# Latent attention: eight of 26 projection units of the next head reserved for places in front of the first output matmuls of the query groups

## The reference, cut to what matters

```python
q = (rmsnorm(c_q, q_norm_g) @ w_uq).reshape(B, S, 8, 128 + 64)      # c_q has 512 features
kv = (rmsnorm(c_kv, kv_norm_g) @ w_ukv).reshape(B, S, 8, 128 + 128)  # c_kv has 256 features
q_nope, q_pe = q[..., :128], q[..., 128:]      # q_pe, k_pe get rotary positions
k_nope, v = kv[..., :128], kv[..., 128:]
s = (q_nope @ k_nope.T + q_pe @ k_pe.T) * 192 ** -0.5               # per head, causal
o = softmax(where(kpos <= qpos, s, -inf)) @ v                        # S = 4096, 8 heads
```

## Time and profile before

| | us |
|---|---|
| median of 3 runs (lowest to highest) | 4792.64 (4781.29 to 4819.37) |
| the profiled execution, its own time | 4795.18 |
| its span, slowest core (core 1) | 4793.2 |
| spans of all cores | 4772.3 to 4793.2 |
| stage 2 in the span, about | 345 to 1027 |

### The profile page before, as it was taken

One profiled execution on the slowest core, in us unless ns is written; L12 is line 12 of the kernel. 1 busy time (PEld: TensorE's weight loads), 2 busy tenths in 40 slices (PEclk: granted clock), 3 DMA queues, 4 the chain that ended last, 5 costly groups with the idle time before them and its releaser, 6 DMA issues.

```text
span 4792.3 us, 76088 instructions; the slowest of 8 cores (4772.3 to 4793.2 us)
## 1 busy us (share of the span) xinstructions
PE 4430.4 (92%) x28892; PEld 2344.1 (49%) x28892; DVE 1692.0 (35%) x2919; ACT 1443.1 (30%) x2431; POOL 124.8 (3%) x211
## 2 busy tenths in 40 slices
PE   5979999975969999599999999999999999999998
PEld 4756666643545555344454444444444444444443
DVE  5632333200212231222566021663124661226641
ACT  4536666630111212112332012432113330123320
POOL 0000000000000000000000000000000000000000
PEclk8879999987989999799999999999999999999999
DMA  8539899799998342154334464445554445644443
GB/s 259 197 66 104 108 108 108 99 176 141 178 160 161 91 115 58 47 170 141 133 137 141 163 220 158 150 154 167 183 195 149 152 145 174 220 158 150 153 137 140
DMA packets 166439, 703.14 MB, mean 147 GB/s; under 512 B 19972, under 2 KB 38692, under 8 KB 150180
## 3 DMA queue, kind: packets, MB, share of 16 engines
q1 hardware_dynamic: 135636, 508.39, 32.3%
q0 software_dynamic: 30448, 189.90, 24.9%
HBM read 783.21 MB, written 138.94 MB: 192 GB/s over the span
## 4 chain that ended last, share of the span: by engine, by line
PE 86%; DMA 4%; DVE 3%; ACT 2%; issue 2%; another core or an unknown queue 2%; SPq 1%; DVEq 0%; POOL 0%; ACTq 0%; POOLq 0%
PE wide L260 79%; PE bank L260 7%; DMA cs<-cosT 2%; ACT pt L269 1%; SPq L74 1%; DVE tm L275 1%; DMA mo<-MOs 1%; DMA wuq<-w_uq 0%; DVE on L484 0%; DVE zacc L272 0%; DMA h<-Hs 0%; ACT zacc L269 0%; DMA x<-xT 0%; PE tbank L695 0%
## 5 line engine op out<-in xcount | busy, mean ns | idle before, releaser
L260 PE MATMUL wide<-h,w 128*128 128x512 bf16 (+1 forms) x11360 | 2104.3, 340 | 141.4 <-DMA h<-Hs 140.1
L260 PEld LDWEIGHTS wide<-h,w 128*128 128x128 bf16 x11360 | 954.5, 97 | 1241.1 <-issue 162.3
L260 PE MATMUL wide<-hid,wd 128*128 128x512 bf16 x2752 | 602.5, 379 | 0.0
L275 DVE SCALAR_TENSOR_TENSOR ac<-u,vecs_sb,ac 128x512 f32<-128x512 f32 x688 | 513.7, 747 | 36.9 <-DVE ac L275 1.4
L269 ACT ACTIVATE ac<-u,vecs_sb 128x512 f32<-128x512 f32 x344 | 280.0, 814 | 648.5 <-DVE u L272 648.4
L260 PEld LDWEIGHTS wide<-hid,wd 128*128 128x128 bf16 x2752 | 269.2, 98 | 324.7
L272 DVE TENSOR_TENSOR u<-wide,rs 128x512 f32<-128x512 f32 (+1 forms) x430 | 250.9, 584 | 382.3 <-PE wide L260 337.0
L272 DVE TENSOR_TENSOR x<-wide,x 128x512 f32<-128x512 f32 (+1 forms) x144 | 89.8, 632 | 739.2 <-PE wide L260 739.2
L536 ACT ACTIVATE pt<-wide,vecs_sb 128x1024 bf16<-128x1024 f32 x256 | 284.5, 1114 | 215.4 <-PE wide L260 204.8
L260 PE MATMUL wide<-qn,kh 128*128 128x512 bf16 (+1 forms) x960 | 311.6, 340 | 4.7 <-DVE vh L447 3.8
L260 PE MATMUL wide<-qp,kpe 128*128 128x512 bf16 (+1 forms) x960 | 309.5, 340 | 2.7 <-issue 2.7
(11 more groups left out here) (140 smaller groups left out, 2939.5 us busy)
## 6 DMA issues: line engine op xcount, KB each, us to landing
w<-w_up_bf SPq DMA_DIRECT2D x344, 512.0 KB, 3.2
h<-Hs SPq DMA_DIRECT2D x64, 1024.0 KB, 14.0
w<-w_gate_bf SPq DMA_DIRECT2D x128, 512.0 KB, 3.3
wd<-w_dn_bf SPq DMA_DIRECT2D x64, 704.0 KB, 4.1
w_up_bf<-w_up POOLq DMA_DIRECT2D x43, 1024.0 KB, 13.7
wd<-w_dn_bf SPq DMA_DIRECT2D x64, 672.0 KB, 3.9
x<-xT SPq DMA_DIRECT2D x16, 2048.0 KB, 9.8
w<-w_out_bf SPq DMA_DIRECT2D x64, 512.0 KB, 3.2
```

The source lines that it names most:

```text
L260: P.op("pe", lambda E: E.matmul(out_ap, lhsT=lhsT_ap, rhs=rhs_ap, start=start, stop=stop, **kw), reads=reads, writes=[out_T])
L275: P.op("dve", lambda E: E.scalar_tensor_tensor(out=out_ap, in0=in0, scalar=scalar, in1=in1, op0=op0, op1=op1), reads=reads, writes=[out_T])
```

## The change

The pace now treats 8 of the 26 units as kept back: it pops while more than 8 are left and as if there were 18 of them. Each entry of `pend` gets a flag, whether it is the first `stage_b` of a query group (or the halo's); in front of one so flagged, up to two units are popped from `fill`. The loop behind the halo step stays as it is.

```diff
-                while fill and len(fill) * total > 26 * (total - stepn):
+                while fill and len(fill) > 8 and (len(fill) - 8) * total > 18 * (total - stepn):
                     fill.pop(0)()
                 while len(pend) > LAG:
-                    pend.pop(0)()
+                    opens, b_step = pend.pop(0)
+                    if opens:
+                        for _ in range(2):
+                            if fill:
+                                fill.pop(0)()
+                    b_step()
...
-                    pend.append(stage_b)
+                    pend.append((kb == 0, stage_b))
...
-            pend.append(halo_b)
+            pend.append((True, halo_b))
             step_end()
             while fill:
                 fill.pop(0)()
             cur = nxt
         while pend:
-            pend.pop(0)()
+            pend.pop(0)[1]()
```

## The result

The changed kernel takes 4898.3 us (median of 6 runs, the lowest 4891.6) against 4806.0 for the kernel before in the same session (lowest 4781.3; its median before the prediction was 4792.6). The ratio is 1.0208, with a 95% interval of 1.0169 to 1.0247: 2.1% slower, forecast were 4900 us and +2.2%. The profiled executions took 4892.6 us against 4795.2, +97, where the sum of the prediction has +108; that the median of 4898.3 comes within 2 us of the 4900 is in part luck.

The account below looks back on a forecast made before the run. TensorE, busy 92% of 4793.2 us, was taken as the bound. 4795 + 55 (burst) + 31 (clock) + 22 (openings) = 4903, forecast as 4900 us, +2.2%; range 4880 to 4925, or 4858 to 4925 including the clock-full case.

Parts of the forecast that it names:

- The count of pops: In the two pop loops: 8 of the units are never taken off the reserve and remain behind each halo step.
- 1, the burst: Behind the halo step of 7 heads: eight left-over units through bank 6, seven uncovered holes of 1.11 us each, +55 us.
- 2, the clock: TensorE's clock falls to half inside and behind each head-end burst, 4.4 us per head, +31 us (bounds 0 to 49).
- the rival of 4870 us: In the head-end bursts the clock stays full, as no single hole is long; 4870 us by median, chance 0.20.
- 3, the openings: At each head's five openings the second unit waits for the first's cast behind the division; +22 us (bounds -21 to +30).
- steps 3 and 13: Openings at these steps of a head: holes grow by 1.1 and 0.7 us, to about 1.1 us each.
- steps 2 and 25: Openings at these steps of a head: holes of 1.27 us become 1.56 and 1.5, +0.3 and +0.2 us.
- 4, what costs nothing: Ordinary steps without a unit, buffers, transfers, queues and VectorE's count of work: no added time.
- Clock full: Rival: TensorE's clock stays full through the head-end bursts; 4872 us, by median 4870, chance 0.20.
- Openings that absorb their units: Rival: paired units lie in existing holes at the openings, none left for a burst; 23 us less, 4770, chance 0.03.
- The smaller loss: Rival: round trip partly hidden or fewer left-over units, openings and half the burst; 4845 us down to no change, chance 0.07.

Follow-up runs that it names:

- e3: Changed kernel with the units behind the halo step rotating over bank 6 and the four score banks; ratio to before 1.0105, stage 2 729.0 us.
- e8: Rerun of the changed kernel with four unused 512-column matmuls added in each of a burst's seven holes; stage 2 765.2 us against 786.7 in the changed kernel.
- e1: Changed kernel without the pops at the openings, leaving the burst alone; stage 2 764.1 us, 81.4 over the kernel before, no ratio.
- e6: Changed kernel with the reserve reduced by each pair, none popped at the halo and none left behind its step; ratio to before 1.0056, stage 2 715.3 us.
- e7: Changed kernel with the old pace and one unit at an opening only where the pace put none; ratio to before 0.9978, stage 2 675.1 us.
- e5: Kernel before, units and pace unchanged, with each group's first output matmuls held back one step more; ratio 0.9962, stage 2 668.9 us.
- e2: Changed kernel with the old pace, nothing kept back, pops at the openings staying; stage 2 721.9 us, 39.2 over the kernel before, no ratio.
- e4: Changed kernel with four 512-column matmuls of unused result added in each of a burst's seven holes; stage 2 764.3 us, 81.6 over the kernel before.

## Why the prediction was right, point by point

- **The count of pops.** Eight value units stand behind each of seven halo steps. It decided the sign and most of the size, and it came from the two conditions alone.
- **1, the burst, +55.** 49 waits of 0.97 us by the profile's counting, each with the 0.16 by which a matmul's record ends behind its last issue: 1.13 x 49 = 55. e3 shows that it is the single bank.
- **2, the clock, +31.** The total was right, its split was not. Taken were a fall 5 us into the burst, 3.4 at the earliest, 1.7 us lost inside and 2.65 behind. Over the 47 bursts whose eight units are all in the traces, the clock fell 0 to 5.0 us behind the first unit, 2.8 in the median; the gaps between units and the last unit took 2.5 us longer than at full clock, and half speed behind them cost 1.7: 4.25 a head, 30 in all, worked out from the starts of the units and the granted clock. In the burst shown above it fell after 1.7 us (507.8 to 509.5) and cost 5.2. The rest of the stage agrees: 104 - 55 - 19 = 30 (the 19 in the next point). e8 gives 21.5; the falls that it still had explain a part of the difference, and the remainder is open.
- The Trainium skill, TensorE: Matmul & The Clock Gate, section "A second HAM failure mode: psum-queue depth-cycling", describes short idles between groups of matmuls of 512 columns, in a kernel that cycles through banks, as enough for the clock to fall (HAM is the page's name for the clock gate). The changed kernel agrees, with groups of 128 columns through one bank: no hole in the bursts was over 1.01 us by the profile's counting, and the clock was 0.50. Its section on HAM oscillation, read as a rule on long gaps alone, would have given the rival of 4870 us.
- **3, the openings, +22.** Two ways to the measured size. The change less e1 is 22.6. By the waits: `kh`, `qp` and `qn` 34.0 us more (42 waits), the division 17.4 less (26), the wait at bank 6 behind the mask products 3.5 less (14, all gone), ScalarE 3.3 more (13). That is 16.4 us, and with 0.16 for each of the 15 waits more it is 19. By parts, steps 3 and 13 were exact, steps 2 and 25 forecast 0.2 to 0.3 too dear.
- **4, what costs nothing.** Two items failed. The wait at bank 6 behind the mask products, 3.5 us before, was left alike and is gone. And TensorE waits for ScalarE's parts at the diagonal 4.3 us instead of 1.0 (17 times instead of 4). Where no unit stands between the steps at the diagonal, the short scores seem to catch up with ScalarE; no run tests that. The two nearly cancel, so that they leave the sum as it was by luck.
- **The rivals.** Clock full: fell with the 0.50 in the windows. What spoke for it, that the clock never fell at the openings before, holds for the core shown; in five others it fell once in mid-stage, in cores 0 and 2 behind a stall of 2.71 us. Openings that absorb their units: e6 draws the eight from the reserve as this rival asks, and it is 32.6 us longer in the stage, not 23 shorter. The smaller loss: all 49 holes of the bursts are there, at the full 1.1 us.

## What to carry to other kernels

Work put into a hole of an in-order engine helps only up to the first piece that must wait for another engine: with one bank between TensorE and VectorE, one unit in the hole shortens the stage (e7) and two lengthen it (e6). A reserve that isn't reduced when it is drawn on comes out somewhere else, so count what is left at the end of a loop before judging where the items were moved to. Where a hole can't be filled with more units, moving the waiting work itself later, behind work that needs nothing (e5), is the better cure.

## What was not expected of the hardware

The clock fell earlier in the bursts than the one stretch of the trace before had suggested: 0 to 5.0 us behind the first unit, where 3.4 was taken as the earliest. It also fell for 3.4 us at a time behind three units in a row in e2, between stretches of dense work, where none was expected. And a burst with 196 added matmuls of no use ran stage 2 21.5 us faster than without them, since TensorE stayed at 2.4 GHz (1.00 in the window against 0.50); this was expected of e4, but of a larger size.
